# A state space layer in chunks of eight tokens, with dense blocks and outputs by token

## The reference, cut to what matters

```python
xn = x * rsqrt(mean(x*x) + EPS) * g_mix                    # norm by token
ug = xn.reshape(n, l, 64 groups, 16 channels)
ab = exp(lam * exp(log_dt)); bb = (ab - 1) / lam * b       # complex, one 64-dim state a group
h[t] = ab * h[t-1] + bb @ ug[t]                            # associative scan over tokens
y = real(c @ h) + d_skip * xn
z = gelu(y);  gl = z @ w_glu + b_glu
h = h + gl[:D] * sigmoid(gl[D:])                           # GLU, then the residual
f = conv_ffn(rmsnorm(h, g_ffn), ...)                       # the layer after it
```

## Time and profile before

| what | us |
|---|---|
| median of 3 runs | 1498.62 (1497.55 to 1498.89) |
| the profiled execution | 1497.03 |
| its span | 1495.2 |
| TensorE busy | 1360.9 (91%) |
| VectorE busy | 807.8 (54%) |
| ScalarE busy | 459.0 (31%) |
| GpSimd busy | 835.4 (56%) |

### The profile page before, as it was taken

One profiled execution on the slowest core, in us unless ns is written; L12 is line 12 of the kernel. 1 busy time (PEld: TensorE's weight loads), 2 busy tenths in 40 slices (PEclk: granted clock), 3 DMA queues, 4 the chain that ended last, 5 costly groups with the idle time before them and its releaser, 6 DMA issues.

```text
span 1495.2 us, 29833 instructions
## 1 busy us (share of the span) xinstructions
PE 1360.9 (91%) x11330; PEld 1308.8 (88%) x11330; DVE 807.8 (54%) x1369; ACT 459.0 (31%) x994; POOL 835.4 (56%) x760
## 2 busy tenths in 40 slices
PE   3337679989999999999999998899999999999998
PEld 2226559989999999999999986599999999999998
DVE  7989982245555555212376876465555555312254
ACT  2234542123443333211124137423434343210021
POOL 4899404654566556655565545355655665655552
PEclk9668889989999999999999999899999999999999
DMA  5010014222332223333355312042223322333231
GB/s 132 3 28 17 13 33 102 85 80 62 95 87 84 84 87 101 89 86 94 93 118 131 95 43 79 16 105 76 85 85 94 87 84 84 102 90 92 81 95 63
DMA packets 233793, 118.14 MB, mean 79 GB/s; under 512 B 34203, under 2 KB 232686, under 8 KB 233658
## 3 DMA queue, kind: packets, MB, share of 16 engines
q1 hardware_dynamic: 223958, 107.31, 25.5%
q10 hardware_dynamic: 9764, 9.84, 3.0%
HBM read 110.84 MB, written 6.09 MB: 78 GB/s over the span
## 4 chain that ended last, share of the span: by engine, by line
PE 83%; DVE 8%; ACT 4%; issue 4%; ACTq 0%; DMA 0%; SPq 0%; DVEq 0%
PE ACC L782 55%; PE MI L782 10%; PE SS L782 8%; PE MI L641 2%; PE SS L750 2%; PE SS L755 2%; PE ACC L732 1%; DVE RSTD L1731 1%; ACT PB L1539 1%; DVE U L1594 1%; PE SS L1073 1%; DVE PB L2046 1%; PE SS L951 1%; ACT BT L1137 1%; ACT CBD L1137 1%
## 5 line engine op out<-in xcount | busy, mean ns | idle before, releaser
L588 POOL TENSOR_TENSOR SPL<-RAW,SPL 128x1024 fp32r<-128x1024 f32 (+2 forms) x172 | 451.0, 2622 | 14.4
L782 PE MATMUL ACC<-NH,SPL 128*128 128x272 f32 x2560 | 438.8, 290 | 5.6 <-DVE NL L1594 4.9
L782 PEld LDWEIGHTS ACC<-NH,SPL 128*128 128x128 f32 x2560 | 366.3, 190 | 7.5 <-issue 6.6
L585 POOL TENSOR_TENSOR TIC<-EPSB 128x1 f32<-128x1 f32 x172 | 37.6, 219 | 555.6 <-PE ACC L782 409.3
L782 PE MATMUL ACC<-NL,SPL 128*128 128x272 f32 x1280 | 265.3, 289 | 0.0
L782 PE MATMUL ACC<-AH,SPL 128*128 128x272 f32 x1408 | 237.5, 289 | 0.0
L782 PEld LDWEIGHTS ACC<-NL,SPL 128*128 128x128 f32 x1280 | 202.4, 190 | 0.0
L782 PEld LDWEIGHTS ACC<-AH,SPL 128*128 128x128 f32 x1408 | 198.9, 188 | 0.2
L586 POOL TENSOR_SCALAR SPL<-RAW 128x1024 fp32r<-128x1024 f32 (+2 forms) x172 | 195.3, 1135 | 0.0
L782 PE MATMUL ACC<-AL,SPL 128*128 128x272 f32 x704 | 145.3, 287 | 0.0
L1594 DVE SCALAR_TENSOR_TENSOR ACC<-WK,CP,ACC 128x560 f32<-128x560 f32 x88 | 70.9, 805 | 97.5 <-ACT ACC L1137 91.1
(11 more groups left out here) (312 smaller groups left out, 2014.8 us busy)
## 6 DMA issues: line engine op xcount, KB each, us to landing
RAW<-in_w_up_dram SPq DMA_DIRECT2D x88, 512.0 KB
RAW<-in_w_down_dram SPq DMA_DIRECT2D x32, 704.0 KB
RAW<-in_w_glu_dram SPq DMA_DIRECT2D x16, 512.0 KB
RAW<-in_w_ple_gate_dram SPq DMA_DIRECT2D x16, 512.0 KB
RAW<-in_w_q_dram SPq DMA_DIRECT2D x16, 256.0 KB
RAW<-in_w_o_dram SPq DMA_DIRECT2D x32, 128.0 KB
UZ<-U SPq DMA_DIRECT2D x128, 17.0 KB, 1.8
XS<-in_x_prompt_dram SPq DMA_DIRECT2D x4, 512.0 KB, 4.9
```

Source lines behind the costliest of these rows:

```text
L585: PIN.tensor_tensor(TIC[:], EPSB[:], EPSB[:], ALU.add)
L588: PIN.tensor_tensor(lo, RAW[:, u, 0:kt, :], hi.bitcast(F32), ALU.subtract).then_inc(sem("split_done"), 1)
L782: last = mm(out[:, h, :], SPL[:, u, w, w0 + k, :], x[:, k0 + k, HT * h:HT * h + HT], start=start and k == 0 and n == 0, stop=stop and k == ...
```

## The change

The recurrence is cut in 64 chunks of eight tokens in place of 128 blocks of four. x is loaded with chunks on the partitions (72 + 8 rows of 8 tokens), so that ScalarE can sum the squares of a token along its row (accum_out) and scale by a per-partition value; TensorE transposes the scaled x to UZ, and U and its regrouping DMAs are gone. g_mix moves into B (BC times G2) and, with d_skip, into a diagonal DG. Within a chunk the layer is a dense 128 x 128 block for each group of 16 channels (KT, 8 x 16 in by 8 x 16 out); its row of taps KKE is made by `kernels` and spread to KT by 128 SBUF to SBUF transfers. Outputs come with chunks on the partitions, gelu works there, and `turn_z` transposes them back to Z. EROT is built by VectorE, C's powers by GpSimd. Scratch lies in RAW, SPL and WK, so GLU's first weights are loaded behind the last of those transfers, and split behind the last scan. The parts of the norm after GLU are made within GLU's loop.

The diff, cut to its core:

```diff
 # SP, ahead of GLU's weights
-                    turn(0, False)
-                    for f in range(KC):
-                        sp.wait_ge(sem("u_ready"), f + 1)
-                        ... 16 sp.dma_start(UZ[...], U[...]) a block
+                    for h in range(2):
+                        sp.wait_ge(sem("uz_made"), len(XG))
+                        sp.wait_ge(sem("kk_ready"), h + 1)
+                        for j in range(CH):
+                            for b in range(8):
+                                sp.dma_start(KT[CG * j:CG * j + CG, NBL // 2 * h:NBL // 2 * h + NBL // 2, :].rearrange(
+                                    "p (f b) n -> p f b n", b=8)[:, :, b, :],
+                                    KKE[CG * b:CG * b + CG, :, CG * (CH - 1 - j):CG * (CH - 1 - j) + P]).then_inc(sem("kt_in%d" % h), 16)
+                    sp.wait_ge(sem("kt_in1"), 16 * CH * 8)
+                    turn(0, False)
 # GpSimd
+            def powers(h):
+                for at0, n, to, row in ((0, 1, 1, A_RE), (0, 2, 2, A2_RE), (0, 4, 4, A4_RE), (4, 1, 8, A4_RE)):
+                    for o in range(2):
+                        for k in range(2):
+                            last = PIN.tensor_tensor(tab[k], CA[...], PR[...] broadcast, ALU.mult)
+                        last = PIN.tensor_tensor(CA[...], tab[0], tab[1], (ALU.add, ALU.subtract)[o])
+            powers(0)
+            ... DEC[:] from R8
+            pool.wait_ge(sem("uz_made"), len(XG))
+            PIN.memset(BD[:], 0.0).then_inc(sem("bd_zero"), 1)
+            powers(1)
+            pool.wait_ge(sem("h_ready"), KC)
 # TensorE
+            for g, (h, b0, n) in enumerate(XG):          # 12 groups, 64 transposes
+                pe.wait_ge(sem("x_scaled"), CH * (h + 1))
+                ... turn(MI[:, g % 2, ...], XN[...], NC_)
+            def turn_b(f): ... 8 transposes of PC, two banks
+            def kernels(h, out): ... 32 products BD x CA and 4 of IDN x DG
+            def inputs(f):                                # 16 products, 64 x 72
+            def outputs(f):
+                pe.wait_ge(sem("kt_in%d" % (f // 4)), 16 * CH * 8)
+                ... y_taken, h0_placed, h_ready
+                for q in range(FQ):
+                    for a in range(2):
+                        mm(SS[0:NU_, a, P * q:P * q + P], UZ[:, 8 * f + 2 * q + a, 0:NU_], KT[:, 8 * f + 2 * q + a, :], ...)
+                    for r in range(2):
+                        for a in range(2):
+                            mm(SS[0:NU_, a, P * q:P * q + P], HSV[rows, par, r, q, 0:NU_], CA[rows, r, FQ * f + q, 1:CH + 1, :], ...)
+            def turn_z(f): ... 8 transposes of ZTK
+            for f in range(KC):
+                if f + 1 < KC: inputs(f + 1)
+                if f: turn_z(f - 1)
+                if f == 1: kernels(1, ACC[:, 2, :])
+                outputs(f)
+            strip("glu", 0, 0)
+            product(0, acc(0), KC - 2, 0, ZH, ZL, True, False, ready="z_split")
+            turn_z(KC - 1)
+            product(0, acc(0), 2, KC - 2, ZH, ZL, False, True, w0=KC - 2, ready="z_split")
+            ... the transposes of FS and VSM, then strip 1
 # ScalarE
+            ... 7 loads of XS on its own queue
+            ... c_turned
+            for j in range(CH):
+                A(junk, XS[0:NC_, j, :], ACT.Square, accum_out=SSQ[0:NC_, j:j + 1])
+            A(RST[0:NC_, :], SSQ[0:NC_, :], ACT.Sqrt, ...).then_inc(sem("rs_root"), 1)
+            ... H from the transposes of XS, H0
+            for g, (h, b0, n) in enumerate(XG):
+                if b0 == NBL // 2 * h:
+                    for j in range(CH):
+                        copy(XN[0:NC_, :, j, :], XS[...], scale=RST[0:NC_, j:j + 1]).then_inc(sem("x_scaled"), 1)
+                copy(UZ[:, b0:b0 + n, :]..., MI[...]).then_inc(sem("uz_done"), 1)
+            ... VEC, CP
+            blocks_b(0); turned_b(0); turned_b(1); kernels(0, SS[:, 1, :]); samples(0)
+            ... turned_b(2), (3), blocks_b(1), turned_b(4) to (7)
+            for f in range(KC):
+                if f + 1 < KC: samples(f + 1)
+                if f: high_z(f - 1)
+                if f == 1: kernels(1, ACC[:, 2, :])      # waits for kk_made and kt_in0, copies into KKE
+                gelu(f)                                   # FS copy, 2 gelus of 72 x 512
-            square("n1", 0, H[:, 0, :], True)
+            high_square("n1", 0, V_GFFN, NH, True)
-            high("n1", "n1", V_GFFN, NH)
 # VectorE
+            ... exponential and angle interleaved, fewer links
+            link(times_power(0, both, ...))
+            dve.wait_ge(sem("rs_root"), 1)
+            for h in range(2):                            # TE in SBUF, EA and PA in PSUM
+                ... times_power of 256, 512 and 1024 elements
+            dve.wait_ge(sem("vec_done"), 1)
+            ... DG
+            for lv in range(6): ... 5 passes on PR
+            dve.wait_ge(sem("uz_made"), len(XG))
+            for lv in range(6): ... EROT, mults of PR and EROT into TE and EA
             def scan(f):
+                ... T1, T2 = ACC * EROT (512), V (2 x 256), 2 scans of 256, back (2 x 512), HSV (2 x 256)
-            with dve.Fori(0, KC - 1) as i:
-                glu(i)
+            with dve.Fori(0, KC - 1) as i:
+                glu(i)
+                low("n1", i, V_GFFN, NH, NL)
                 add_squares("n1", i)
-                    lows(norm, V_GFFN, NH, NL)
```

More of the change, by code:

```diff
@@ L98, in constants @@
         c[row, C_BM + 32 + row // STEPS % RQ] = 1.0
+    for row in range(P):
+        c[row, C_MSK + row % CG] = 1.0
     c[0, C_SEL:C_SEL + 64] = 1.0
@@ new lines, in outputs, with turn_z @@
+                last.then_inc(sem("y_made"), 1)
+            def turn_z(f):
+                pe.wait_ge(sem("y_taken"), f + 1)
+                if f >= 2:
+                    pe.wait_ge(sem("z_split"), f - 1)
+                if f == 1:
+                    pe.wait_ge(sem("kk_taken"), 2)
+                for i in range(CH):
+                    last = turn(ZB[f % 2][:, i // 4, NU_ * (i % 4):NU_ * (i % 4) + NU_], ZTK[0:NU_, i, :], NU_)
+                last.then_inc(sem("z_turned"), 1)
+            turn_b(0)
@@ L759, in _ @@
+            turn_b(1)
+            kernels(0, SS[:, 1, :])
+            inputs(0)
+            for f in range(2, KC):
+                turn_b(f)
             for f in range(KC):
-                prep(f)
-                inputs(f)
+                if f + 1 < KC:
+                    inputs(f + 1)
                 if f:
-                    outputs(f - 1)
-            outputs(KC - 1)
-            pe.wait_ge(sem("fs_ready"), 1)
-            for r in range(2):
-                turn(MI[0:PAIRS, 1, P * r:P * r + P], FS[:, r, :], P)
-                for h in range(2):
-                    last = turn(MI[:, 0, P * (2 * r + h):P * (2 * r + h) + P],
-                                VSM[:, r, 4 * h:4 * h + 4, :].rearrange("p b q -> p (b q)"), P)
@@ new lines, in _, with blocks_b @@
+            act.wait_ge(sem("vec_made"), 1)
+            copy(VEC[:], ACC[:, 0, 0:V_N]).then_inc(sem("vec_done"), 1)
+            act.wait_ge(sem("cp_made"), 1)
+            copy(CP[:].rearrange("p l v c -> p (l v c)"), ACC[:, 1, 0:352]).then_inc(sem("vec_done"), 1)
+            def blocks_b(h):
+                act.wait_ge(sem("bd_zero"), 1)
+                act.wait_ge(sem("pc_ready"), h + 1)
+                pairs = slice(PAIRS // 2 * h, PAIRS // 2 * h + PAIRS // 2)
+                for a in range(2):
+                    rows = slice(64 * a, 64 * a + 64)
+                    last = copy(BD[rows, :, pairs, CG * a:CG * a + CG].rearrange("p r q c -> p q r c"), PC[rows, pairs, :, CH - 1, :])
+                last.then_inc(sem("bd_ready"), 1)
+                act.wait_ge(sem("bd_ready"), h + 1)
@@ L1276, in _ @@
-            gelu(KC - 1)
+                    act.wait_ge(sem("z_turned"), f)
+                out = ZTK[0:NU_].rearrange("p i (q a c) -> p a q i c", a=2, c=CG)
+                for a in range(2):
+                    last = A(out[:, a], SS[0:NU_, a, :].rearrange("p (q i c) -> p q i c", q=FQ, i=CH), ACT.Gelu_apprx_tanh)
+                last.then_inc(sem("y_taken"), 1)
+            blocks_b(0)
+            turned_b(0)
+            turned_b(1)
+            kernels(0, SS[:, 1, :])
+            samples(0)
```

856 lines of the change are left out of this document (454 added, 402 removed).

## The result

| | before | after |
|---|---|---|
| median of 14 runs each, us | 1498.03 (1496.03 to 1499.20) | 1493.61 (1490.73 to 1496.12) |
| ratio, 95% interval | | 0.9972, 0.9963 to 0.9980 |
| span of the profiled execution, us | 1495.2 | 1491.9 |

A forecast was written before the change was run, and what follows sets the result against it. TensorE was taken as full except in a 226 us front set by VectorE, then ScalarE and TensorE in turns, and a 4.85 us hole. 13.9 - 2.5 + 7.5 = 18.9 us off gave 1478.1, as median 1480; range 1455 to 1502.

The forecast's parts named there:

- step 1: Start, SP's queue: C's loads stand fourth, two issues more ahead of them put c_turned at 23 us (22.0 before).
- Step 2 and 3: Front, ScalarE: squares of x, root and copies of H until 44 us, then scaling and turning x; VEC at 69.
- step 6: Front, VectorE: 58 passes, partly slowed beside GpSimd's powers; EROT done at 117 us, scan(0) gives h_ready at 123.5.
- Step 7: Front, SP: dense blocks in two halves of 64 transfers at 0.65 us; landed at 121 and 179.4, 22 us wait between.
- Rivals B and C: Dense-block transfers: B (0.15), they don't bind, 1460 us; C (0.12), they cost with their rows, 1525 at 1.0 us pitch.
- Steps 8 to 10: Front's end: outputs(4) to (7) at 8 us a turn, GLU's weights hidden, first GLU strip ends at 218.6: -13.9 us.
- Step 11: Behind GLU's first strip: ScalarE's copies, nine issues and the sigmoid now follow it in place of lying beside it: +2.5 us.
- Step 12: Norm after GLU: high and low parts made under the gates remove the hole and half clock at the up strip: -7.5 us.
- Rival D: Preamble: ScalarE's steps 2 and 3 or VectorE's contention with GpSimd run 12 to 18 us over, 1492 to 1498; chance 0.13.

The follow-up runs named there:

- B last: Changed kernel with SyncE's loads of B moved behind C's and x issued once log_dt has landed: 1485.16 us, 0.9922.
- x after C: Changed kernel with ScalarE issuing the loads of x only when C has landed: 1493.81 us, 0.9979.
- x after B: Changed kernel with ScalarE issuing the loads of x only when B has landed: 1490.18 us, 0.9950.

## Why the prediction was wrong

The direction was right and the size was not. By the steps of the prediction:

| step | forecast, us | measured, us |
|---|---|---|
| 1: c_turned | 23 | 39.65 |
| 2, 3: squares to VEC | 23 to 69 (46) | 39.55 to 82.6 (43) |
| 6: EROT done | 117 | 124.3 |
| 7: half 0, from VEC to its first issue | 8.5 | 12.7 |
| 7: pitch of a transfer | 0.65 | 0.64 |
| 7: half 0 landed, half 1 landed | 121, 179.4 | 138.5, 199.2 |
| 8: one turn of outputs(4) to (7) | 8 | 6.57 |
| 8: last outputs end | 208.4 | 226.1 |
| 10: GLU's first strip ends | 218.6 | 234.15 |
| 11: behind the first strip | +2.5 | +3.1 |
| 12: norm after GLU | -7.5 | -7.0, undone +7.9 |

**The step that failed is step 1**: "C's loads are the fourth thing on SP's queue; two issues more ahead of them ... put c_turned at 23 us", with its companion, "That x is loaded from 0.8 us on ScalarE's queue is worth nothing by itself". I had put the loads in order on their queue and priced their issues, and had taken a load on another queue as free. Both queues feed the same 16 DMA engines, and those were full, at 85 to 133% up to 18 us. What the runs showed in its place: c_turned came at 39.65 us, B's second issue stalled for 19.2 us beside x and for 2.34 with x moved behind C, and x itself took 19 us and not the 5 that its old rate gives. The slip at c_turned is 16.6 us, that at the end of GLU's first strip 15.5, that in the gain 14.2 (18.6 forecast, 4.4 measured). That the first two are so near is in part luck: other terms nearly cancel on the way. Up to half 0's first issue ScalarE's copies give back 3.0 us and the rest loses 4.2; behind it half 0's transfers make -0.3, the time between the halves +2.3 (60.7 for 58.4), outputs(4) to (7) -2.1 (26.9 for 29) and GLU's first strip -2.2 (8.0 for 10.2). What ties the slip to the time is the experiment with B last: 7.7 us off the start took 8.4 off the end. The prediction had the material for it. The table of issues gave the issue times of B and C, and I read from it what SyncE does and not what the DMA engines do; windows of the profile before have B's loads alone at a DMA share of 1.24 and 1.07 (4 to 8 us, 120 and 90 GB/s). The Trainium skill, "DMA: Bandwidth & Descriptors", section "Queues, rings and completion order", states that each DMA engine takes turns between the queues, a whole packet at a time; the trace fits, in that B's longest packet record went from 307 to 2640 ns and its loads landed 20.7 and 23.4 us after their issue in place of 5.0 and 7.2. The order of turns itself no run here shows.

My second mistake lies under the first. Even with the sharing in mind I would have put x at 5 us, from its 406 to 424 GB/s before. It takes 18.4 to 19.4 us from its first packet to its last in the changed kernel, with x after C, with x after B and with B last. The four loads into 56 partitions ran at half the old rate, which makes about 11 us of it; the three loads into eight partitions, a fifth of the bytes, make the other 8 to 9. The experiment with x after C showed it by failing: the expected 11 us did not come, and with 4 KB rows a packet took 299 ns in place of 159.

**Step 2 and 3, step 6**: right, and the uncertain ones in my own list. ScalarE's forty copies took 3 us less than forecast. The 58 VectorE passes beside GpSimd ended 7.3 us after the forecast with a start that was 13.6 late, so they took 6 less. The mechanism was seen as described: one pass of 32 elements waited for GpSimd's, its neighbour did not (timelines of VectorE and of GpSimd):

```profile
99.17 0.19 DVE L1864 TENSOR_TENSOR PR<-PR 128x32 f32<-128x32 f32 x1
99.28 2.35 DVE L1865 TENSOR_TENSOR PR<-PR 128x32 f32<-128x32 f32 x1
```
```profile
95.33 3.76 POOL L585 TENSOR_TENSOR TAB<-CA,PR 128x1024 f32<-128x1024 f32 x2
99.17 2.41 POOL L588 TENSOR_TENSOR CA<-TAB 128x1024 f32<-128x1024 f32 x1
```

**Step 7** was the largest term and came out nearly to the digit: 0.64 from issue to issue, the wait of 22.5 us at outputs(4) where 22 was forecast. What it took too short is TensorE's kernels(0): 6.3 us and not 2.5, with 64 products of 0.42 us each at the median. SyncE's issues of the changed kernel (shortest, median and longest in ns, first and last start):

```profile
L486 SPq DMA_DIRECT2D KT<-KKE x128: 585/595/1572, 95.3 to 197.2; - x128
```

That the transfers bind, and by their issues, is now shown from three sides: started earlier (-16.0), spread over two queues (-13.0 more), doubled (+82). Rivals B and C are both out. Two slips of the working changed nothing in the sum: 68.5 + 6 + 2.5 + 0.7 is 77.7 and not 77.5, and the chain of the kernel before has VectorE's powers, B's powers and then the norm's U up to 84 us, with the recurrence's scans only behind that.

**Steps 8 to 10** followed: the turns were 1.4 us shorter each, GLU's weights were hidden, as GLU's first product started right behind the last outputs. **Step 11** was 0.6 low. **Step 12** was right, and the experiment that undid it puts 7.9 us on it and shows that the parts cost the loop nothing.

**Rival D** had the place and the size (12 to 18 us, 1492 to 1498) and the wrong cause: I named ScalarE's copies and the passes beside GpSimd, which both ran shorter than forecast. The sum was made with one link missing, at the very start, where the profile before has no second load beside B to show it.

What stays open: B last leaves the squares at 31.9 us, where C still lies beside x. That x would be fast if it were spread over both halves of the partitions was not tried, so the partitions written are not parted from the distance of the rows read. Nor was half 0 tried on two queues, and what makes the products of kernels(0) take 1.10 us a group in some kernels and 0.67 in others at the same granted clock is not known.

## What to carry to other kernels

Price a load twice: once as an issue on its queue, and once as time on the DMA engines that all queues share, at the rate of its own shape (here a load into half as many partitions ran at half the rate, one into eight partitions slower still), beside whatever else is loading then. At the start of a kernel put the loads in the order in which their users come, and leave the one with a later user (B here) behind. Where short transfers stand in a row on the path, count them: here each cost 0.64 us on one queue, with 16 KB as with 32 KB, and starting them earlier and giving a part to a second queue were both worth their full time.

## What was not expected of the hardware

- Loads of x into 56 partitions, with next to nothing beside them, ran at 193 to 208 GB/s in windows of 4 us, with the DMA engines 90 to 95% busy (x after C, and with rows of 4 KB), 424 into 128 partitions before; a 4096 B packet took 299 ns in place of 159. Rows of 32 KB into 8 partitions took 3.6 to 4.8 us a packet at the median, 6.8 to 9.1 B/ns.
- log_dt, 64 numbers of 4 B issued at 2.95 us, landed at 23.0 beside x and B, and at 4.9 with x behind C.
- The stall showed at another issue than that of the load that was moved, on the other queue: 19.2 us at B's second half with x from the start, 26.1 over C's first eight with x behind log_dt.
- Transfers of 32 KB from SBUF to SBUF take 0.595 us to issue on SyncE's queue and 0.617 on ScalarE's at the median, both at once without slowing one another.
- A group of sixteen products of kernels(0) took 1.10 us in some kernels and 0.67 in others, both at a granted clock of 1.00.
